# Attention products with V cut into single slots and spread over the loop, in a two-layer hybrid trunk

## What is computed

```python
p_s = masked_softmax(jnp.einsum("bqgrd,bgqkd->bgrqk", q_r, k_g) * scale, smask)
o_s = jnp.einsum("bgrqk,bgqkd->bqgrd", p_s.astype(v_g.dtype), v_g)
...
p_w = masked_softmax(jnp.einsum("bqgrd,bkgd->bgrqk", q_r, kb) * scale, wmask)
o_w = jnp.einsum("bgrqk,bkgd->bqgrd", p_w.astype(vb.dtype), vb)
return (gt[..., 0:1] * o_c + gt[..., 1:2] * o_s + gt[..., 2:3] * o_w).astype(q.dtype)
```

## Time and profile before

| what | value |
|---|---|
| median of 3 runs | 1373.88 us (1373.64 to 1375.7) |
| the profiled execution's own time | 1373.7 us |
| its span, first to last instruction | 1371.9 us |
| granted TensorE clock | 1.00 |
| TensorE busy | 1361.3 us, 99% |
| VectorE, ScalarE, GpSimd busy | 616.5, 507.4, 618.9 us |

### The profile page before, as it was taken

The page is one execution under the profiler, slowest core; times in us unless marked ns, Lnnn a source line. Parts: engine busy times, 40 slices in busy tenths (PEclk is TensorE's granted clock), DMA queues, the critical chain, the costliest instruction groups (busy, mean ns, idle before and its releaser), DMA issues.

```text
span 1371.9 us, 19145 instructions
## 1 busy us (share of the span) xinstructions
PE 1361.3 (99%) x7952; PEld 1147.5 (84%) x7952; DVE 616.5 (45%) x1006; ACT 507.4 (37%) x873; POOL 618.9 (45%) x334
## 2 busy tenths in 40 slices
PE   8999999999999999999999999999999999999999
PEld 7998987788888888888879999887888888888887
DVE  6638577723344213442165395766234442144421
ACT  5564336634322122222346442456342231132210
POOL 4467317643444344443344663266444444344442
PEclk9999999999999999999999999999999999999999
DMA  7326200124332243333222442010323322433222
GB/s 183 105 73 141 80 8 1 32 63 100 92 92 92 85 115 92 92 101 107 85 92 66 114 125 62 1 31 4 87 67 110 105 85 85 120 95 92 92 85 85
DMA packets 178582, 114.70 MB, mean 84 GB/s; under 512 B 46144, under 2 KB 161088, under 8 KB 178496
## 3 DMA queue, kind: packets, MB, share of 16 engines
q1 hardware_dynamic: 176384, 113.22, 29.0%
q10 hardware_dynamic: 2112, 0.26, 0.1%
HBM read 109.80 MB, written 3.67 MB: 83 GB/s over the span
## 4 chain that ended last, share of the span: by engine, by line
PE 94%; DVE 3%; POOL 1%; issue 1%; DMA 0%; ACT 0%; SPq 0%; DVEq 0%
PE ps L667 71%; PE ps L1030 6%; PE ps L779 2%; PE ps L974 2%; PE ps L957 2%; PE ps L931 2%; DVE att L2028 1%; PE ps L705 1%; PE ps L983 1%; POOL arena L1604 1%; PE ps L759 1%; PE ps L892 1%; PE ps L609 1%; PE ps L810 0%; DMA x_tok<-in_x 0%
## 5 line engine op out<-in xcount | busy, mean ns | idle before, releaser
L1525 POOL TENSOR_TENSOR w_lo<-w_raw,w_hi 128x2048 fp32r<-128x2048 f32 (+3 forms) x97 | 439.1, 4527 | 595.2 <-ACT w_hi L1185 547.4
L1185 ACT ACTIVATE w_hi<-w_raw 128x2048 fp32r<-128x2048 f32 (+3 forms) x99 | 186.7, 1885 | 557.4 <-PE ps L667 519.9
L667 PE MATMUL ps<-hT_hi,w_lo 128*128 128x512 f32 x928 | 231.2, 391 | 0.0
L667 PE MATMUL ps<-hT_hi,w_hi 128*128 128x512 f32 x896 | 224.3, 392 | 0.0
L667 PE MATMUL ps<-hT_lo,w_hi 128*128 128x512 f32 x896 | 222.7, 390 | 0.0
L667 PEld LDWEIGHTS ps<-hT_hi,w_lo 128*128 128x128 f32 x928 | 173.3, 188 | 35.8 <-issue 0.3
L667 PEld LDWEIGHTS ps<-hT_lo,w_hi 128*128 128x128 f32 x896 | 167.7, 188 | 35.0 <-issue 0.3
L667 PEld LDWEIGHTS ps<-hT_hi,w_hi 128*128 128x128 f32 x896 | 166.7, 188 | 34.3 <-issue 0.4
L2080 DVE TENSOR_TENSOR aT_lo<-ffn_tmp,aT_hi 128x512 fp32r<-128x512 f32 x44 | 142.1, 3229 | 30.7 <-ACT aT_hi L1195 30.7
L2143 DVE TENSOR_TENSOR ffn_tmp<-ps,ffn_tmp 128x512 f32<-128x512 f32 x44 | 30.4, 692 | 243.7 <-ACT ffn_tmp L1486 243.7
L2152 DVE SCALAR_TENSOR_TENSOR x_tok<-ps,st,x_tok 128x512 f32<-128x512 f32 x32 | 24.0, 750 | 175.4 <-PE ps L667 175.4
(11 more groups left out here) (326 smaller groups left out, 1811.3 us busy)
## 6 DMA issues: line engine op xcount, KB each, us to landing
w_raw<-in_w_gate_up SPq DMA_DIRECT2D x88, 512.0 KB, 5.0
w_raw<-in_w_in SPq DMA_DIRECT2D x19, 1024.0 KB, 5.2
w_raw<-in_w_down SPq DMA_DIRECT2D x16, 1024.0 KB, 5.0
w_raw<-in_w_down SPq DMA_DIRECT2D x8, 768.0 KB, 4.4
w_raw<-in_w_out SPq DMA_DIRECT2D x16, 256.0 KB, 3.8
w_raw<-in_w_out SPq DMA_DIRECT2D x8, 512.0 KB, 4.7
w_raw<-in_w_in SPq DMA_DIRECT2D x2, 1120.0 KB, 5.4
w_raw<-in_w_in SPq DMA_DIRECT2D x2, 1056.0 KB, 7.1
```

Of the source, the lines that this page charges most:

```text
L667: mm = nc.tensor.matmul(out_ap, a(ab, k), b(bb, k), start=first and i == 0, stop=last and i == len(kts) - 1)
L1185: nc.scalar.activation(whi[:, c % 2, 0:kt * w], raw[:, c % 2, 0:kt * w], ACT.Copy).then_inc(S["w_hi"], 1)
L1525: nc.gpsimd.tensor_tensor(wlo[:, c % 2, 0:kt * w], raw[:, c % 2, 0:kt * w], whi[:, c % 2, 0:kt * w].bitcast(F32), ALU.subtract).then_inc(S ...
```

## The change

`pv` takes a slot in place of a third. In six iterations, from iteration 6 on, it takes 2, 1, 1, 1, 1 and 0 slots: slots k - 6 and k - 5 when k % 6 == 0, slot k - 5 otherwise, none when k % 6 == 5. The last three slots stay together in iteration 27. The semaphore `pv` now counts slots, and the waits on it are rewritten: a copy into a `pT` buffer waits for the slot that last used it, and the split of weight chunk 13, whose destination holds some of these buffers, waits for slot 20 as before.

```diff
@@ pv @@
-            def pv(v):
+            def pv(k):
+                v, s = divmod(k, 3)
                 p, br = divmod(v, 2)
-                if v == 0:
+                if k == 0:
                     pe.wait_ge(*S.at("cadd", 4, l))
-                elif br == 0:
+                elif k % 6 == 0:
                     pe.wait_ge(*S.at("mix_lo", p, l))
-                for s in range(3):
-                    k = 3 * v + s
-                    pe.wait_ge(*S.at("pTd", k + 1, l))
-                    pe.wait_ge(*S.at("pTa", k + 1, l))
...
+                pe.wait_ge(*S.at("pTd", k + 1, l))
+                pe.wait_ge(*S.at("pTa", k + 1, l))
...
+            def pv_at(k):
+                if k == N_SLOTS + 3:
+                    return 21, 22, 23
+                if k < 6 or k == N_SLOTS + 2:
+                    return ()
+                return ((k - 6, k - 5), (k - 5,), (k - 5,), (k - 5,), (k - 5,), ())[k % 6]
@@ loop @@
-                if k >= LAG_PV and k % 3 == 0:
-                    pv(k // 3 - 2)
+                for q in pv_at(k):
+                    pv(q)
@@ evacuate, on ScalarE and on VectorE @@
-                    act.wait_ge(*S.at("pv", k // 3 - 1, l))
+                    act.wait_ge(*S.at("pv", k - 5, l))
@@ split of chunk 13 @@
-                    act.wait_ge(*S.at("pv", 7, l))
+                    act.wait_ge(*S.at("pv", 21, l))
```

More of the change, by code:

```diff
@@ L26 @@
 N_PARAMS = 16
-LAG_TRANSPOSE, LAG_PV = 3, 6
+LAG_TRANSPOSE = 3
 N_SLOTS = 24
@@ L63 @@
     "norm_gains": 16, "ffn_gains": 16, "oS": 4, "rb": 1, "rbps": 1, "rstd0": 1, "rstd1": 1, "rbt": 1, "rbtps": 1, "rb2": 1, "unscaled": 2, "og": 4, "ogT": 2, "ored": 1, "oroot": 1, "osq": 1, "pTa": 24, "pTd": 24,
-    "params": 160, "pscaled": 48, "ptr": 48, "pv": 8, "qdec": 1, "qhi": 4, "qkmask": 1, "qkn": 1, "qlo": 4, "qn": 4,
+    "params": 160, "pscaled": 48, "ptr": 48, "pv": 24, "qdec": 1, "qhi": 4, "qkmask": 1, "qkn": 1, "qlo": 4, "qn": 4,
     "qnT": 4, "qnps": 4, "qps": 4, "qred": 4, "qrms": 1, "qseed": 1, "qsq": 4, "roped": 1, "scan": 1, "score": 24,
@@ L958, in p_transpose @@
                     mm.then_inc(S["ptr"], 1)
-            def pv(v):
+            def pv(k):
+                v, s = divmod(k, 3)
                 p, br = divmod(v, 2)
-                if v == 0:
+                if k == 0:
                     pe.wait_ge(*S.at("cadd", 4, l))
-                elif br == 0:
+                elif k % 6 == 0:
                     pe.wait_ge(*S.at("mix_lo", p, l))
-                for s in range(3):
-                    k = 3 * v + s
-                    pe.wait_ge(*S.at("pTd", k + 1, l))
-                    pe.wait_ge(*S.at("pTa", k + 1, l))
[L970 to L976, removed]
-                mm.then_inc(S["pv"], 1)
+                pe.wait_ge(*S.at("pTd", k + 1, l))
+                pe.wait_ge(*S.at("pTa", k + 1, l))
+                pieces = ((0, 0, 2, 0), (1, 1, 1, 2)) if s == 0 else tuple((s + 1, j, 1, j) for j in range(s + 2))
+                for i, j, n, b in pieces:
+                    for g in range(NG):
+                        rows, v0 = slice(g * HEAD, (g + 1) * HEAD), br * 256 + P + g * HEAD
+                        mm = nc.tensor.matmul(ps[rows, 6, i * P:(i + n) * P], kv[:, j, v0:v0 + HEAD],
+                                              pT_of(k, g)[:, b * P:(b + n) * P],
+                                              start=br == 0 and i == 0 and j == 0, stop=False, skip_group_check=True)
+                mm.then_inc(S["pv"], 1)
+            def pv_at(k):
[4 more added lines that the diff above has]
+                return ((k - 6, k - 5), (k - 5,), (k - 5,), (k - 5,), (k - 5,), ())[k % 6]
             def cmp_pv(p):
@@ L2037, in evacuate @@
                 if k >= 6:
-                    dve.wait_ge(*S.at("pv", k // 3 - 1, l))
+                    dve.wait_ge(*S.at("pv", k - 5, l))
                 V.tensor_copy(pT_of(k, 0), ps[:, 4, 0:width(k % 3)]).then_inc(S["pTd"], 1)
```

## The result

The changed kernel takes 1378.54 us (median of 7 runs, 1378.29 to 1379.98), the kernel before beside it 1373.82 (7 runs, 1373.62 to 1375.7). The ratio is 1.0033 with a 95% interval of 1.0023 to 1.0044: slower by 4.7 us, where 3.3 were forecast. The whole interval lies above the 0.2% that was taken as what a measurement can tell.

A forecast was written before the change was run, and what follows sets the result against it. TensorE's instruction stream plus its waits was taken as the bound. 0.33 + 1.34 = 1.67 us a layer, 3.3 in all, took the profiled 1373.7 to 1377.0; with 0.2 to the median, 1377.2 us, range 1374.8 to 1379.4.

The forecast's parts named there:

- Ahead of scores, 0.14 a run: Iterations 8, 14, 16, 19, 20, 22: each new run costs 0.14 us beside its passes, 0.84 for six.
- Ahead of the recurrence, 0.23 a run: Iterations 7, 10 and 13: each new run costs 0.23 us beside its passes, 0.69 together.
- Ahead of the projection, 0.32: Iteration 25: the new run costs 0.32 us beside its passes.
- The waits of iterations 9 and 15: TensorE's transposes there stop waiting, saving 0.33 and 0.75 us, together 1.08 a layer.
- The wait that comes back in iteration 16, 0.3: TensorE reaches iteration 16's transposes sooner and waits 0.3 us for ScalarE's copy of slot 12; 0 to 0.5 possible.
- Up to `gdn_out`, 0.33 later: Up to iteration 18, new runs 1.11, less 1.08, plus 0.3: `gdn_out` starts 0.33 us later a layer.
- The pin by GpSimd: Iteration 22: `gdn_out` starts when GpSimd is done; TensorE's savings after VectorE's last root become waiting, about 1 us.
- Behind it, 1.34: After `gdn_out`'s wait: slot 17's passes with their run, 1.02, plus iteration 25's run, 0.32, add 1.34 us a layer.
- What was said to be hidden: Chunk 13's split moves by one run, 1.0 us, covered by two more iterations and their products before the projection needs it.
- GpSimd doesn't pin: Rival at iteration 22: all removed waits count, 0.26 us a layer, 1374.4; chance 0.32 together with the lower switch bound.
- The switches are covered: Rival on the new runs: they fill only time TensorE waited; free switches give -1.59 us a layer, 1370.7; chance 0.04.
- Nothing is gained: Rival: VectorE and ScalarE stay late, so the 1.08 stays; 2.75 us a layer, 1379.4; chance 0.10.

The follow-up runs named there:

- experiment 2: Changed kernel with no products in iterations 7 and 13, slots 2 and 8 joining the next slot's run: 1376.81 us, ratio 1.0021 to before in the median of 1.0022.
- Experiment 4: Changed kernel with slot 20's products moved to iteration 24 beside slots 18 and 19, none in iteration 25: 1377.76 us.
- kernel 5: Kernel before (thirds), but slot 3's products taken alone in iteration 8 and slot 9's in iteration 14: 1372.52 us, ratio 0.9988.
- experiment 1: Changed kernel with slot 17's products ahead of the delta rule's output transposes in iteration 22 instead of behind them: 1376.72 us.
- 3: Changed kernel with the delta rule's output transposes one iteration later, in 23 and 24: 1376.42 us.
- kernel 6: Kernel before (thirds), but slots 3, 9 and 15 taken alone in iterations 8, 14 and 20: 1372.3 us, ratio 0.9987.
- 7: Kernel before (thirds), slots 3, 9 and 15 taken alone in iterations 8, 14 and 20, output transposes in iterations 23 and 24: 1371.05 us.

## Why the prediction was right, and where its sizes were off

The forecast was 1377.2 us, and 1378.54 lies in its range of 1374.8 to 1379.4. The three parts of its mechanism hold: the runs cost more than the waits that they cover, a new wait comes in iteration 16, and GpSimd pins iteration 22. But one of its own signs of being wrong came true as well: runs that cost over 0.25 us more than their passes.

**Ahead of scores, 0.14 a run: right.** Eight passes take 0.80, which is 0.66 + 0.14; sixteen take 1.02, which is 0.88 + 0.14.

**Ahead of the recurrence, 0.23 a run: too small, 0.34 or 0.35.** This is the term of the sum that was mis-sized. Going in costs 0.10 and the run 0.14, as forecast, but what comes behind it was not in the sum: the first whole-array product after a run takes 0.55 in place of 0.44. The trace of before already had it, and the prediction overlooked it. The recurrence's product L994 follows the transposes in iteration 10 and a third in iteration 12, and L1002 in iteration 4 follows a wait. The timeline of TensorE before:

```profile
208.00 0.71 PE L1002 MATMUL ps<-arena 128*128 128x128 f32 x4 [0.18 <-DVE arena L2048]
...
230.48 0.61 PE L994 MATMUL ps<-state,arena 128*128 128x128 f32 x4
...
239.94 0.71 PE L994 MATMUL ps<-state,arena 128*128 128x128 f32 x4
```

Behind a run the product lasts 0.71 in place of 0.61. It does so behind a wait without any run too, so this part need not be the price of a switch: in these rows it is paid where the product doesn't follow other whole-array work at once.

Three such runs make 0.33 us a layer more than forecast; experiment 2 measured two of them, 0.70. These three runs and that of iteration 25 are the ones above 0.25; the last was so in the forecast itself, at 0.32. The Trainium skill's page "TensorEngine Tiling (Array Packing)", section "Tiling Modes", says that a change of mode drains the engine. The rows agree that a run costs more than its passes, on the way in and on the way out; but 0.34 us is some three times the 0.11 that two changes would cost by the estimate of 0.053 each that the prediction took from the Trainium skill's page "TensorE: Matmul & The Clock Gate", Part 2. No run here separates the change of mode from other losses between two kinds of products.

**Ahead of the projection, 0.32: about right.** From L957 to the projection's product the rows give 0.75 + 1.02 = 1.77, less 0.57 and 0.88 for the passes: 0.32. The projection's first product behind the run takes 0.03 more. Experiment 4 gave 0.40 and 0.37.

**The waits of iterations 9 and 15: right,** as the rows of the result show, and right that they were worth having: kernel 5 takes them with two runs in place of ten and wins 0.90 and 0.85 us in the two layers, near 1.08 less two times 0.14.

**The wait that comes back in iteration 16, 0.3: right,** 0.35 (1.10 less 0.75), and on ScalarE's copy. The timeline of ScalarE in the changed kernel has

```profile
251.63 0.51 ACT L1201 ACTIVATE idle_w<-ps 128x384 f32<-128x384 f32 x1
```

It ends at 252.14, and the second half of the transposes starts at 252.29: 0.15 later, the 0.14 or so that the prediction added between a copy and what waits for it.

**Up to `gdn_out`, 0.33 later: 0.77 measured.** L1024 starts at 271.81 in place of 270.65; less the 0.39 by which the stage starts later, that is 0.77. It is GpSimd's end that moved so far, and before it VectorE's last root: the timeline of VectorE has in the changed kernel

```profile
261.54 0.48 DVE L2079 SCALAR_TENSOR_TENSOR st<-st 128x16 f32<-128x16 f32 x1
```

in place of 260.36, 1.18 later and 0.79 without the 0.39. So the delay arises ahead of iteration 18, where the three runs at the recurrence (0.33) and iteration 16 (0.05) lie. Another 0.05 are a small new wait: iteration 7's transposes take 0.80 until the products (218.32 to 219.12) where iterations 9 and 15 have 0.75 and 0.76. That leaves 0.01. The term was forecast at less than half its size, because it is what is left when 1.08 is taken from 1.41: small errors in the large terms are large in the difference.

**The pin by GpSimd: right.** Experiments 1 and 3 each take it away in another manner and win 0.92 and 1.05 us a layer; 6 and 7 show the saving of iteration 21 vanish with it and come back without it. Its wait was forecast as about 1 us and reads 0.83 as idle time. The row understates it: from the mask to L1024 it is 2.24 us where 0.12 + 0.66 would do, 1.46 of waiting. Of that 0.48 is a wait of the transposes themselves, ahead of the pin: experiment 1 shows it alone, 0.23 from mask to transposes and 1.12 from there to the products, for 0.12 and 0.75. The other 0.98 is the pin. It is a little less than the 1.02 of the run that experiment 1 puts there, so TensorE then comes somewhat later than GpSimd, and that experiment wins 0.92 and not 1.02.

**Behind it, 1.34: 1.42 measured** (2.19 less 0.77). The run with slot 17's passes is 1.03 (272.39 to 273.42) and that of iteration 25 is 0.35 by rows, with the product behind it, so 0.04 is unplaced.

**What was said to be hidden: right.** The projection's first product of iteration 25 starts 2.55 us later than before (286.26 for 283.71), and L609 at the stage's end 2.58 later. No wait for the split of chunk 13 comes in between.

**The sum.** 0.77 + 1.42 = 2.19 us a layer for 1.67 forecast, and 4.4 a kernel for 3.3. Of the 0.52 a layer that the forecast lacks, 0.33 is the product behind the run, 0.05 iteration 16, 0.05 iteration 7 and 0.03 the projection's product; 0.06 are small pieces not placed. All of them point the same way, so no luck of opposite errors is in the result. The medians differ by 4.7, and 0.3 of them are outside what the stages show; the interval of the ratio, 3.2 to 6.0 us, is wider than that.

**The rivals.** "GpSimd doesn't pin" falls with experiment 1. "The switches are covered" falls with the rows: no new run costs less than 0.14. "Nothing is gained" falls with iterations 9 and 15, and with kernel 5.

**Slips of arithmetic, none of which moves the forecast.** The runs of iterations 19 and 20 lie in the stretch that the pin swallows, so cheaper switches save on eight runs and not on ten. With the lower bound the sum is then 1.27 us a layer (1376.4 us) and not 1.17, and with the estimated 0.053 a switch it is 1.5 us in all and not 1.1. Without the pin the ten runs break even at 1.59 us by the prediction's own terms, and not at 1.3. The chances of its parts add up to 0.37 for the same time and 0.59 for slower, and not to 0.35 and 0.61.

## What to carry to other kernels

Before work is spread out to fill waits, price the switch that each new piece brings, where it stands: here the same run cost 0.14 us ahead of one kind of work and 0.34 between two of another, and ten of them outweighed waits of 1.08 us a layer. One piece ahead of each wait did the same good with two runs in place of ten.

Then look for the next place where the engine waits for one that does not depend on it, and for the point from which that one works by itself (here VectorE's last root in iteration 18). Time saved between that point and the wait is lost, as kernel 6 shows; time saved ahead of the point counts, as kernel 5 shows; and work moved behind the wait is paid in full. Moving the waiting instruction itself (here one iteration later, 0.37 to 1.05 us a layer, by how much had gone into the wait) is what turns the savings into time.

## What was not expected of the hardware

The first whole-array product behind a run of 64-column products took 0.55 us until the next in place of 0.44, in addition to what the run itself costs: this part is paid behind the run, in a row that doesn't look like part of it. The same product is as slow behind a wait.

GpSimd's pieces of one shape differ in length. In the changed kernel's timeline of GpSimd:

```profile
263.48 1.06 POOL L1618 TENSOR_TENSOR arena<-arena,st 128x256 f32<-128x256 f32 x1
...
267.68 0.61 POOL L1618 TENSOR_TENSOR arena<-arena,st 128x256 f32<-128x256 f32 x1
```

The first has 0.45 us more. At the same time VectorE runs an operation with two inputs, both in SBUF, the on-chip memory that GpSimd's piece reads too:

```profile
263.33 0.73 DVE L2086 TENSOR_TENSOR aT_lo<-arena,aT_hi 128x512 fp32r<-128x512 f32 x1
```

The Trainium skill's "GPSIMD Engine Reference" names such contention in the table of its section "Specifications"; the two rows agree with it, and put a size to it in this place. In the kernel before a piece of L1612 (262.38, 0.62 us) also overlaps VectorE's L2080 and isn't longer; there it is VectorE's operation, started later (262.65), that takes 0.90 in place of 0.68. So GpSimd isn't always the one that pays. No run here took VectorE's operation away, so that it is the cause is argued, not shown. Since GpSimd sets the start of `gdn_out`, it would be the next thing to try in a kernel that keeps the output in iteration 22.
